# A two-block transformer kernel on one core: parts of h made straight from PSUM, the first weight group split a stage earlier, squares of x behind the parts, new attention sequences

## What is computed

```python
def first_block(...):            # per layer
    h = rms_norm(x, norm1_g[l]) * (1.0 + sc1) + sh1
    proj = h @ w_in[l]
    ...                          # differential attention, gated delta rule
    x = x + gt1 * (merged @ w_out[l])
    h = rms_norm(x, norm2_g[l]) * (1.0 + sc2) + sh2
    x = x + gt2 * (jnp.square(jax.nn.relu(h @ w_mlp1[l])) @ w_mlp2[l])

def second_block(...):           # per layer
    proj = rms_norm_2(h, attn_norm[l]) @ w_in[l]
    ...                          # neighbourhood, latent and window attention, group norms
    h = h + o @ w_out[l]
    h = h + expert_choice_ffn(rms_norm_2(h, ffn_norm[l]), w_router[l], w_gate[l], w_up[l], w_down[l])
```

## Time and profile before

| | us |
|---|---|
| median of 3 runs | 2210.61 |
| lowest and highest run | 2209.35, 2215.11 |
| the profiled execution, its own time | 2210.75 |
| its span, first to last instruction | 2209.4 |
| TensorE busy | 1894.3 (86%) |
| VectorE busy | 910.3 (41%) |
| ScalarE busy | 632.4 (29%) |

### The profile page before, as it was taken

One profiled execution on the slowest core, in us unless ns is written; L12 is line 12 of the kernel. 1 busy time (PEld: TensorE's weight loads), 2 busy tenths in 40 slices (PEclk: granted clock), 3 DMA queues, 4 the chain that ended last, 5 costly groups with the idle time before them and its releaser, 6 DMA issues.

```text
span 2209.4 us, 31133 instructions
## 1 busy us (share of the span) xinstructions
PE 1894.3 (86%) x12904; PEld 1264.6 (57%) x12904; DVE 910.3 (41%) x1528; ACT 632.4 (29%) x1090; POOL 43.2 (2%) x46
## 2 busy tenths in 40 slices
PE   6999999999999999999899856666799897666666
PEld 3887888987888889987655311112276552212112
DVE  3675575645576676645763100000058530000001
ACT  3244235534245235534451100000055310000001
POOL 0001000000002000000000000000000000000000
PEclk9999999999999999999999988887899999888878
DMA  9565348556533354554448999999983689999997
GB/s 338 208 229 192 116 153 305 191 191 232 187 143 126 122 185 153 191 190 107 192 177 357 427 427 425 428 427 428 418 242 145 280 358 426 427 426 426 428 427 330
DMA packets 119990, 617.50 MB, mean 279 GB/s; under 512 B 18432, under 2 KB 21418, under 8 KB 86570
## 3 DMA queue, kind: packets, MB, share of 16 engines
q1 hardware_dynamic: 119274, 613.85, 70.3%
q10 hardware_dynamic: 576, 1.66, 0.2%
HBM read 614.44 MB, written 1.05 MB: 279 GB/s over the span
## 4 chain that ended last, share of the span: by engine, by line
PE 58%; DMA 28%; DVE 8%; ACT 3%; issue 1%; SPq 1%; POOL 0%; DVEq 0%; ACTq 0%
PE pb L701 56%; DMA ring<-in_w_up_dram 17%; DMA ar<-in_w_up_dram 4%; DMA hT<-in_w_up_dram 3%; PE pb L704 2%; DMA ring<-in_w_down_dram 2%; DVE ar L1651 2%; DVE ar L1643 1%; DMA ring<-in_w_in_dram 1%; DVE small L1659 1%; DVE ar L1647 1%; ACT ar L2412 1%; DVE ar L1655 1%; DVE small L1647 0%; ACT hT L2412 0%
## 5 line engine op out<-in xcount | busy, mean ns | idle before, releaser
L701 PE MATMUL pb<-ring,ar 128*32 128x512 f32 (+1 forms) x2128 | 363.5, 727 | 184.3 <-DMA ring<-in_w_up_dram 142.2
L701 PE MATMUL pb<-ar 64*64 64x64 f32 (+10 forms) x3760 | 435.9, 370 | 74.3 <-DMA hT<-in_w_up_dram 33.9
L2416 ACT COPY ar<-pb 128x512 f32<-128x512 f32 (+2 forms) x195 | 112.8, 579 | 919.5 <-PE pb L701 869.9
L1655 DVE COPY ar<-pb 128x512 f32<-128x512 f32 (+5 forms) x98 | 58.7, 599 | 720.7 <-PE pb L701 705.4
L701 PEld LDWEIGHTS pb<-ar 64*64 64x64 f32 (+5 forms) x3760 | 210.7, 144 | 240.9 <-issue 221.2
L701 PEld LDWEIGHTS pb<-ring,ar 128*32 128x32 f32 (+1 forms) x2128 | 97.6, 132 | 396.4 <-issue 385.4
L701 PE MATMUL pb<-hT,ring 128*128 128x256 f32 x1024 | 236.3, 387 | 0.4 <-ACT ar L2412 0.4
L701 PEld LDWEIGHTS pb<-hT,ring 128*128 128x128 f32 x1024 | 193.8, 193 | 33.8 <-issue 7.8
L1643 DVE TENSOR_TENSOR ws<-ring,ws 128x1024 fp32r<-128x1024 f32 x128 | 156.9, 1226 | 123.5 <-ACT ws L2416 122.0
L701 PE MATMUL pb<-hs,ws 128*128 128x256 f32 x1536 | 186.3, 283 | 4.9 <-ACT hs L2416 2.4
L701 PEld LDWEIGHTS pb<-hs,ws 128*128 128x128 f32 x1536 | 184.7, 192 | 7.0 <-issue 2.3
(11 more groups left out here) (163 smaller groups left out, 1644.9 us busy)
## 6 DMA issues: line engine op xcount, KB each, us to landing
ring<-in_w_down_dram SPq DMA_DIRECT2D x46, 2048.0 KB, 28.1
ring<-in_w_gate_dram SPq DMA_DIRECT2D x42, 2048.0 KB, 28.2
ring<-in_w_up_dram SPq DMA_DIRECT2D x40, 2048.0 KB, 23.4
ring<-in_w_mlp_dram SPq DMA_DIRECT2D x32, 2048.0 KB, 7.8
ring<-in_w_in_dram SPq DMA_DIRECT2D x28, 2048.0 KB, 10.5
ring<-in_ada_w_dram SPq DMA_DIRECT2D x24, 2048.0 KB, 8.3
ar<-in_w_gate_dram SPq DMA_DIRECT2D x12, 2048.0 KB, 20.3
ar<-in_w_up_dram SPq DMA_DIRECT2D x12, 2048.0 KB, 23.5
```

What stands on the lines that cost most here:

```text
L701: return e.matmul(o, l, r, start=start, stop=stop)
L1655: return e.tensor_copy(o, i)
L2416: return e.copy(o, i)
```

## The change

- `hT_out` is gone from these hand-overs. ScalarE makes the high parts straight from the banks of PSUM (`h_high_a`, `h_high_b`, `parts`). VectorE makes the low parts: in block 2 in one instruction from PSUM (`h_low_b`), in block 1 and "n2" by way of a float32 copy (`h_full_a`, `full`), since block 1's later products read that copy. ScalarE writes the copy of part 3 itself. Part 1 is read by VectorE first, the others by ScalarE first.
- The weights of group 0 go to memory of their own (`w_first`) and are split in front of the last addition to x, except for the first projection of all. In layer 1 of block 2 their block is loaded in two halves, with a semaphore for the first.
- In both layers of block 2 the squares of x and the wait for their root move behind the parts, into groups 0, 1 and 3 of the projection; the load of `c2` moves with them.
- In block 1 three modulation rows stand in front of the transposes and one behind, not two and two.
- `SPARE` loses the fillers at "n1" and in the projections of block 2, and at "n2" goes from 2 and 10 to 0 and 6.
- Both sequences of the attention of block 2 are new from the scores on; what each step does is unchanged, and so are the fillers inside.

Shared parts and TensorE (of the sequences only the end of layer 0):

```diff
-    ("turn", "n1"): (0, 2), ("turn", "n2"): (2, 10), ("lin", "a"): (4, 0), ("lin", "b", 0): (3, 3), ("lin", "b", 1): (4, 4),
-    ("lin", "b", 2): (2, 2), ("l_cqT",): (7, 7), ("l_mT", 0): (7, 7), ("v_pv", 0): (2, 2), ("v_pv", 2): (1, 1), ("z_route", 1): (1, 1),
+    ("turn", "n2"): (0, 6), ("lin", "a"): (4, 0), ("l_cqT",): (7, 7), ("l_mT", 0): (7, 7), ("v_pv", 0): (2, 2), ("v_pv", 2): (1, 1), ("z_route", 1): (1, 1),
...
-        ("q_stat", 5), ("c_copy", 13), ("c_copy", 14), ("y_x", 1, 2), ("y_x", 1, 1), ("t_turn", 15), ("o_w", 1, 3),
-        ("v_pv", 7), ("q_stat", 6), ("y_x", 1, 3), ("w_out", 6), ("c_copy", 15), ("w_out", 7), ("q_stat", 7),
...
+        ("y_x", 1, 2), ("c_copy", 14), ("e_exp", 15), ("q_stat", 5), ("y_x", 1, 1), ("t_turn", 15), ("q_stat", 6),
+        ("w_out", 6), ("v_pv", 7), ("c_copy", 15), ("w_out", 7), ("q_stat", 7), ("o_w", 1, 3), ("o_w", 2, 0),
+        ("o_w", 2, 2), ("y_x", 1, 3), ("o_w", 2, 1), ("r_root", 2), ("y_x", 2, 0), ("y_x", 2, 2), ("z_sq", 0),
...
+        w_first = [zone_r(o, 1024) for o in (0, 1024)]
...
+        def w_parts(site, l, g):
+            return w_first if (site, l) != ("a", 0) and g == 0 else wp[g % 2]
...
-        sqr, sqr_out2, sqr_end = xn[:, 512:1024], zone(17920, 512), zone(1024, 512)
+        sqr, sqr_out2, sqr_end = xn[:, 512:1024], zone(17920, 512), zone(3136, 512)
...
-            def turned(site, l, ks, cps=range(4)):
-                for cp, k in zip(cps, ks):
-                    psum.until(k, A if cp % 2 else V, "hT", site, l, cp)
-            def lin3(site, l, ns, ahead):
+            def turned(site, l, ks):
+                for cp, k in enumerate(ks):
+                    psum.until(k, V, "h_lo", site, l, cp)
+            def lin3(site, l, ns):
...
-                    spare(l, *(("lin", site, g) if site == "b" else ("lin", site) if g == 0 else ()))
+                    spare(l, *(("lin", site) if site == "a" and g == 0 else ()))
...
-                    hi, lo = [v4(z[:, 0:2 * n], 2) for z in wp[g % 2]]
+                    hi, lo = [v4(z[:, 0:2 * n], 2) for z in w_parts(site, l, g)]
...
-                    for i in range(2):
+                    for i in range(3):
...
-                    for i in range(2, 4):
-                        ada_row(1, 0, i)
+                    ada_row(1, 0, 3)
...
-                    for i in range(2):
+                    for i in range(3):
...
-                    for i in range(2, 4):
-                        ada_row(1, 1, i)
-                turned("n1", l, ks)
-                group = lin3("a", l, [512, 512, 512], ahead(l))
+                    ada_row(1, 1, 3)
+                turned("a", l, ks)
+                group = lin3("a", l, [512, 512, 512])
...
-                ahead(l)(3)
...
-                turned("an", l, turn("an", l, ("moe", 0) if l else ("mlp", 1)))
-                steps = dict(x_lin=lin3("b", l, [512, 512, 512, 288], lambda j: None), x_out=lambda l, j: projected("b", l, j, (V, A)),
+                turned("b", l, turn("an", l, ("moe", 0) if l else ("mlp", 1)))
+                steps = dict(x_lin=lin3("b", l, [512, 512, 512, 288]), x_out=lambda l, j: projected("b", l, j, (V, A)),
```

VectorE (of `lin3` only its head is shown as removed):

```diff
+            def mean_square(squares):
...
+            def norm_r(squares):
+                mean_square(squares)
...
-            def lin3(site, l, ns, first, ahead, hT_of, between=lambda: None):
...
+            def w_low(site, l, g):
+                j, q = g // 4, g % 4
+                name, n = ("win" if site == "a" else "win2", l, j), 512 if j < 3 else 288
+                hi, lo = [v4(z[:, 0:2 * n], 2) for z in w_parts(site, l, g)]
+                e.wait_ge(*A("w_hi", site, l, g))
+                tt(lo, W(name)[:, 2 * q:2 * q + 2, :], hi, ALU.subtract).then_inc(*V.up("w_lo", site, l, g))
+                if q == 3:
+                    let_go[name] = V, "w_lo", (site, l, g)
+            def h_full_a(l, cp):
+                e.wait_ge(*(P("turn", "n1", l, cp) if cp == 1 else A("h_hi", "a", l, cp)))
+                for j in range(2):
+                    cc = 2 * cp + j
+                    m = ts(hT3[:, cc, :], ps("turn", "n1", l, cp)[:, 256 * j:256 * j + 256], sa1[:, cc:cc + 1], modT2[l][:, cc:cc + 1],
+                           ALU.mult, ALU.add)
+                    m.then_inc(*(V.up("hT", "n1", l, cp) if j else step()))
+            def h_low_a(l, cp):
+                if cp in (0, 2):
+                    h_full_a(l, cp)
+                e.wait_ge(*A("h_hi", "a", l, cp))
+                d = slice(2 * cp, 2 * cp + 2)
+                tt(hp[1][:, d, :], hT3[:, d, :], hp[0][:, d, :], ALU.subtract).then_inc(*V.up("h_lo", "a", l, cp))
+            def h_low_b(l, cp):
+                e.wait_ge(*A("h_hi", "b", l, cp))
+                for j in range(2):
+                    cc = 2 * cp + j
+                    m = stt(hp[1][:, cc, :], ps("turn", "an", l, cp)[:, 256 * j:256 * j + 256], pcol(pc[l]["an"] + cc), hp[0][:, cc, :],
+                            ALU.mult, ALU.subtract)
+                    m.then_inc(*(V.up("h_lo", "b", l, cp) if j else step()))
...
+                def whole(cp):
+                    return v4(aux[:, 512 * (cp % 2):512 * (cp % 2) + 512] if cp < 3 else xn[:, 1024:1536], 2)
+                def full(cp):
+                    e.wait_ge(*(P("turn", "n2", l, cp) if cp == 1 else A("h_hi", "n2", l, cp)))
+                    for j in range(2):
+                        cc = 2 * cp + j
+                        m = ts(whole(cp)[:, j, :], ps("turn", "n2", l, cp)[:, 256 * j:256 * j + 256], sa2[:, cc:cc + 1],
+                               modT2[l][:, 24 + cc:25 + cc], ALU.mult, ALU.add)
+                        m.then_inc(*(V.up("h_full", l, cp) if j else step()))
...
-                    tt(hs[1][:, d, :], v4(aux[:, 512 * (cp % 2):512 * (cp % 2) + 512], 2), hs[0][:, d, :], ALU.subtract).then_inc(*V.up("h_lo", "n2", l, cp))
+                    tt(hs[1][:, d, :], whole(cp), hs[0][:, d, :], ALU.subtract).then_inc(*V.up("h_lo", "n2", l, cp))
...
-                for cp in range(4):
-                    if cp % 2 == 0:
-                        hT_out("n2", l, cp, lambda cc: sa2[:, cc:cc + 1], lambda cc: modT2[l][:, 24 + cc:25 + cc],
-                               lambda cc: aux[:, 256 * (cc % 2):256 * (cc % 2) + 256])
-                    if cp:
-                        parts(cp - 1)
+                full(1)
+                full(0)
+                parts(0)
+                parts(1)
+                full(2)
+                parts(2)
...
+                w_low(*(("b", 0, 0) if l else ("a", 1, 0)))
...
+                h_full_a(l, 1)
+                h_low_a(l, 0)
+                if l == 0:
+                    w_low("a", l, 0)
+                h_low_a(l, 1)
+                w_low("a", l, 1)
...
+                    if g < 2:
+                        h_low_a(l, g + 2)
+                    if g + 2 < 12:
+                        w_low("a", l, g + 2)
...
+                squares = ("moe", 0) if l else ("mlp", 1)
+                if l:
+                    w_low("b", l, 0)
+                h_low_b(l, 0)
+                h_low_b(l, 1)
+                w_low("b", l, 1)
+                h_low_b(l, 2)
+                h_low_b(l, 3)
+                def group(g):
+                    if g + 2 < 16:
+                        w_low("b", l, g + 2)
+                    if g == 1:
+                        mean_square(squares)
+                    if g == 3:
+                        e.wait_ge(*G("root", *squares))
```

ScalarE and SP:

```diff
+            def squares(site, l, wait=True, some=range(4)):
+                for i in some:
...
-            def lin3(site, l, ns, first, ahead, hT_of):
...
+            def w_high(site, l, g):
+                j, q = g // 4, g % 4
+                name, n = ("win" if site == "a" else "win2", l, j), 512 if j < 3 else 288
+                if (site, l, g) == ("b", 1, 0):
+                    e.wait_ge(*D("win2_first"))
+                elif q == 0 or (site, l, g) == ("b", 1, 2):
+                    e.wait_ge(*landed(name))
+                if g > 2 or (site, l, g) == ("a", 0, 2):
+                    e.wait_ge(*P("lin", site, l, g - 2))
+                copy(v4(w_parts(site, l, g)[0][:, 0:2 * n], 2), W(name)[:, 2 * q:2 * q + 2, :]).then_inc(*A.up("w_hi", site, l, g))
+            def h_high_a(l, cp):
+                e.wait_ge(*(V("hT", "n1", l, 1) if cp == 1 else P("turn", "n1", l, cp)))
+                for to in (hT3, hp[0]) if cp == 3 else (hp[0],):
+                    for j in range(2):
+                        cc = 2 * cp + j
+                        m = act(to[:, cc, :], ps("turn", "n1", l, cp)[:, 256 * j:256 * j + 256], ACT.Identity, scale=sa1[:, cc:cc + 1],
+                                bias=modT2[l][:, cc:cc + 1])
+                        m.then_inc(*(step() if j == 0 else A.up("hT", "n1", l, cp) if to is hT3 else A.up("h_hi", "a", l, cp)))
+            def h_high_b(l, cp):
+                e.wait_ge(*P("turn", "an", l, cp))
+                for j in range(2):
+                    cc = 2 * cp + j
```

(80 more changed lines are left out.)

166 lines of the change are left out of this document (43 added, 123 removed).

## The result

The changed kernel took 2194.73 us (median of 4, 2194.07 to 2198.84) against 2211.63 (median of 4, 2209.35 to 2215.11): ratio 0.9922, 95% interval 0.991 to 0.9935. The profiled execution has a span of 2193.3 us against 2209.4, 16.1 less; the forecast said 20.5 less. The prediction counted from the execution of 2210.75 us, so its 2190.3 is to be set against 2194.73.

A forecast was written before the change was run, and what follows sets the result against it. Expert stages were taken as bound by DMA transfers, with the hand-overs counting one for one. 6.8+6.3+1.4+2.1+2.0+1.2-0.8+1.5 = 20.5 us won from 2210.75 gave 2190.3; range 2183 to 2199.

The forecast's parts named there:

- Block 2, 6.8 and 6.3: Projection of block 2: group 3 done 6.8 us earlier in layer 0 and 6.3 us earlier in layer 1.
- Block 1, layer 1, 1.4: Projection of block 1, layer 1: group 3 at 546.5 against 547.9, 1.4 us won; modulation products covered most old wait.
- First projection, 2.1: First projection of all: group 3 ends at 48.4 against 50.5, 2.1 us won.
- Group 3 ends at 48.4 with the reduced clock below counted: First projection: end of its group 3, slow clock included, against 50.5 before.
- Hidden layer 0, 1.2: Hand-over n2, layer 0: 1.2 us won, with a third modulation row delaying the transposes by 0.9.
- Layer 0 has the same steps: Hand-over n2: layer 0 priced by layer 1's steps, with a third modulation row in front; 1.2 us won.
- Hidden layer 1, 2.0, and clock, 0.8: Hand-over n2, layer 1: 2.0 us won by earlier parts, 0.8 lost to a clock drop after fewer fillers.
- New sequences, 1.5: Attention of block 2, both layers: reordered steps win 1.5 us, with 4 either way for the unpriced rest.
- Both waits go: Attention of block 2: TensorE's waits for VectorE's copy before the scores of head 4, 1.02 and 1.59 us, disappear.
- Handoffs eat half: Rival: latency between engines halves the six hand-over terms; 9.5 us won, 2201; chance 0.10.
- The SP queue: Rival, block 2: later squares delay 16 bias-table gathers and everything behind them on SP; 2215 to 2220 us, chance 0.02.
- no effect: Rival: the expert stages or a hidden DMA bound take all the gain; 2210 us, chance 0.03.

The follow-up runs named there:

- Experiment 11: Changed kernel with weight group 2 split in front of part 3 of h in block 2, on both engines; 2194.55 us, ratio 0.9922.
- Experiment 5: Changed kernel with the first weight group of block 2 and of block 1, layer 1 split in its own stage again; 2199.28 us, ratio 0.9942.
- b_all_root: Changed kernel, block 2 with whole h, first weights split in the stage, squares in front, root's wait before low weight 1; 2206.0 us, ratio 0.9973.
- squares_front: Changed kernel with all four squares of x back in front of the parts of h in block 2; 2199.25 us, ratio 0.9941.
- Experiment 3: Changed kernel with modulation rows two and two again in the hidden layer of layer 0; 2194.76 us, ratio 0.9926.
- experiments 1 and 2: First: changed kernel with the old attention sequences, 2194.04 us, ratio 0.9919. Second: kernel before with only the new sequences, 2212.2 us, ratio 1.0001.

## Why the forecast held, and where its terms were off

**Block 2, 6.8 and 6.3: right, measured 6.35 and 5.31.** The steps hold: early split, parts from PSUM, nothing late behind them. In layer 0 the four groups took 11.45 from their first product to the mark, where the sum had 10.7. In layer 1 the missing 1.0 is mostly in VectorE's chain, which begins with the subtraction that "delays everything behind it there by that much": from 1597.70 to the end of low weight 2 at 1606.05 its instructions (three of 1.23, eight of 0.53) are 7.9 us long and took 8.35, and low parts of 1.05 for two instead of 1.0 add 0.2; the last twenty products took 4.86 from their first to the mark, where the sum had 4.6. Experiment 11 shows that this chain binds. By single edits, parts straight from PSUM are the largest piece (3.8), then the squares behind them (1.8), the root's wait (1.2, 1.2, and 1.1 and 1.0 in the kernel before), the early split (1.4 and 0.7).

**Block 1, layer 1, 1.4: right in sign, measured 0.93.** TensorE was busy for 27.93 of 28 us from 524 to 552 before, and for the same from 522 to 550 after; so only the filler products (1.13) and the order could give anything. Experiment 5 shows what let them go: without them and without the early split the hand-over is back at 20.13, with a bare wait in their place.

**First projection, 2.1: mis-sized, measured 0.45.** The step that failed is "Group 3 ends at 48.4 with the reduced clock below counted". Its own terms without a slow clock give 48.1 (low weight 0 at 37.7, group 1 at 42.2, low weight 2 at 43.6, group 2 at 45.4), so the slow stretch was counted at 0.3; and low weights 0 to 2 came 0.5 to 0.7 later than laid out. What both cost shows in the kernels that share this code. From the end of the instruction that makes the scale (`sa`) to the cast that marks group 3, the changed code took 15.69 and 15.70 us in the two whose clock did not fall here (`b_all_root`, `squares_front`), 16.28 to 16.57 in the seven that lost 1.4 to 1.7 us to it (16.55 in the changed kernel itself), 17.78 and 17.82 in the two that lost 3.0 to 3.1. The row of 39 to 42 us, changed kernel and then `squares_front`:

```profile
39.00:42.00 3.00, 3.00 (x9) 2.33 (x9) 2.71 (x4) 2.72 (x5) 0.00 (x0) 0.57 1.06 389
39.00:42.00 3.00, 2.96 (x13) 2.46 (x14) 2.66 (x4) 2.71 (x6) 0.00 (x0) 1.00 1.06 390
```

So the clock cost 0.85 here and not 0.3, about half of the 1.6 us that TensorE lost, and the chain without it 15.7 and not the 14.8 of the sum (48.1 less 33.3). The comparison itself is uncertain, too: the code of the kernel before took 17.26, 17.85 and 18.02 in its three kernels. The means are 17.7 before and 16.6 after, 1.1 won; the 0.45 of this pair of traces is on the low side, 0.26 of it because the scale was ready later (33.55 against 33.29).

**Hidden layer 0, 1.2: mis-sized, measured 0.31.** "Layer 0 has the same steps" was the fault: it has the same steps, but TensorE was never idle there before (15.00 busy of 15.00 from 333 to 348): the two modulation rows behind the transposes (3.64) cover the making of the parts, and making them faster could not help. Only the filler products (1.13) left. They had filled the wait for the norm; the third row fills it now, and of what that gives, 0.62 goes to the fourth row's wait for its DMA. Experiment 3 measures it.

**Hidden layer 1, 2.0, and clock, 0.8: net 1.2, measured 1.41, but for other reasons.** The drop came and cost 0.1 (experiment 3); the parts themselves gave 1.5 and not 2.0, and low parts 0 to 3 were ready 0.2 to 0.4 later than laid out, again hand-overs counted without a gap. That the net came out near 1.2 is luck: two errors of 0.5 and 0.7 against each other.

**New sequences, 1.5: wrong; 0.36 in this pair of traces, and no gain clear of the spread** (experiments 1 and 2). "Both waits go" was right for the waits and wrong for the time: in layer 0 another took its place.

**What the forecast did not have:** 1.37 from the shorter slow stretch at 75 us. It is nothing that the edit did, and it offset part of the shortfall of 5.0 in the hand-overs; 4.4 us remain between 2190.3 and the median. That the total is as near as this is partly luck.

**Rivals.** "Handoffs eat half": the six terms fell short by a quarter (14.8 of 19.8), by gaps, the clock and the full TensorE of layer 0 together. (Half of them, with the clock and the sequences as forecast, would have been 10.6 won and not the 9.5 that the rival names.) The SP queue and "no effect" did not come up. The stages of experts kept their length to 0.3 of 421 and 0.1 of 427.

## What to carry to other kernels

Before a hand-over is priced by how much earlier its parts are made, look at whether the engine that waits for them is idle at all, and at what its filler products cover. Where TensorE was full with fillers counted, little came (0.3 and 0.9); where it waited, the chain laid end to end was right to 1 us in 6. Lay the chain with the gaps of the rows between dependent instructions (0.45 on 7.9 us here). A stage whose clock may or may not fall has no single length: read it in several kernels that share its code before a gain under 1 us is believed. A wait that an order makes disappear is worth nothing until the sum of all waits in the stage has fallen.

## What the runs showed of the hardware

- What the low clock costs depends on the waits around it: 0.1 us in front of the hidden layer (experiment 3), where TensorE lost 1.7 and its slower products ran inside waits; 0.85 of 1.6 in the first projection of the changed kernel, against kernels that share the code and kept the full clock there.
- The same code at the same place got the low clock in one kernel and not in another, after the same 1.9 us of idle (0.55 against 1.00 in 824 to 827). Losses summed from 30 to 1180 us were 9.4 to 16.2 us over the fourteen kernels, one trace each, and mostly came in portions of 1.4 to 1.7 us, or twice that, at one place. Between runs of one kernel there is a hint of the same: over the 43 runs of the kernel before beside the experiments, the longer ones tend to have the lower mean granted clock (correlation -0.38 to -0.74 in the three sets). That would be some third of their spread; the rest is open, and it was not tested by itself.
- TensorE can fall to 0.50 while it is shown busy all the time: in the kernel before at 75.0 us, during 32 products of 16 columns, in the changed one at 75.7, just behind them. In four kernels with the same products it did not fall there. By the Trainium skill (TensorE: Matmul & The Clock Gate, Part 1) the gate follows how busy the array has recently been and knows two levels; the levels agree with the traces, where no stretch is below 0.50. Why it fell while the rows show TensorE busy, no run here shows.
